# Delta pairs in slots: a pair's recurrence and the front of the next but one beside the inversion levels of the pair between

## The chip, the cores and the metric

The kernel runs on one core of a Trainium2 chip. The metric is the device time of one execution in microseconds (us). The engines are PE (TensorE; PEld is its weight load), DVE (VectorE), ACT (ScalarE), POOL (GpSimd) and SP (SyncE, which issues most of the DMAs). Each runs its own instructions strictly in the order of the program, and they meet only at semaphores.

## The reference, cut to what matters

One inference step of a two-layer decoder trunk runs over 1024 prompt tokens and eight sample tokens. The stage that the change is mainly about is the gated delta rule of the second layer: 8 heads, 64-token chunks, a 128x128 state per head. For each chunk it computes

```
m     = strict_lower(kb @ k^T * exp(gcum_i - gcum_j))
tinv  = inverse(eye + m);  u = tinv @ (v * beta);  w = tinv @ (kb * exp(gcum))
aqk   = lower(q @ k^T * exp(gcum_i - gcum_j))
v_new = u - w @ s
o     = (q * exp(gcum)) @ s + aqk @ v_new
s     = s * exp(g_last) + (k * exp(g_last - gcum))^T @ v_new
```

and then an rms norm of o times silu(z), and the output projection. Only s passes from chunk to chunk. The eight sample tokens make one step of the same rule on states of their own, which are read and written whole (4 MB). The first layer has an RWKV-7 recurrence of the same build (chunks of 64, an inversion, a state H), whose decay and gates are sigmoids.

## The kernel before

The kernel is a row of phases, one after the other: norm, projections, attention, `rwkv_phase`, an output projection (`residual_phase`), a convolutional feed-forward, norm, projections (`odd_phase`), `delta_phase`, `delta_samples_phase`, `residual_phase` again under the name `out1`, and a second feed-forward. The pages of the samples' attention are read and multiplied beside most of the first phases.

`delta_phase` takes the 16 chunks as 8 pairs; the two chunks of a pair lie in the partitions 0 to 63 and 64 to 127. Each engine has one loop over the pairs, and one body of the loop is one pair from start to end. A pair has three parts.

- The **front** loads q, k, v (`dn_x`), squares them (L2158), sums the squares with a matmul of ones (L2092), takes Ln and Exp for the norm (L2160, L2163), spreads the gates over partitions with a matmul (L2097), forms kb, kbe and qe on DVE (L2203 to L2206), transposes k and v (L2102), forms the decay differences (L2214 to L2220), `dn_bv` and `dn_ktm` (L2223, L2225), multiplies the three Gram blocks (L2112) and masks them (L2230 to L2240).
- The **levels** are the inversion: five times a group of 16 matmuls `y` (L1377), a copy on ACT (L1402), two such groups `z` and `zt` (L1388, L1394; the last level has only `zt`) and two subtractions on DVE (L1414, L1417). POOL multiplies the five masks (L2084) into a ring of five buffers.
- The **recurrence** goes twice, once for each chunk (`p`): kbe times state (L2129, semaphore `w_done`), state times qe (L2132), a subtraction on DVE (L2246, `r_ready`), the product with the inverse (L2137), a copy on ACT (L2179), the state's update (L2142 on PE, L2251 and L2254 on DVE), the output's part (L2145). Then the output is copied and squared (L2182, L2184), summed (L2150), normed (L2186, L2188, L2257) and multiplied with z into `T.h` (L2260).

`T.h` stays in SBUF until `out1` reads it. `delta_samples_phase` starts when `delta_phase` has ended: a load of the sample rows and the states, a turn through DRAM, two multiplications with a reduction each over 128 x 64 elements on DVE, another turn through DRAM, and a store of the states.

`rwkv_phase` is a loop over 8 pairs too, with the samples' pages as filling on DVE, ACT and PE. `prep_act` and `prep_dve` form the gates of a pair: Exp on ACT, then 1 + x and a reciprocal on DVE, for the pair `th`, `sg` (L1563 to L1566) and for the pair `rw`, `ra` (L1579 to L1582). The recurrence on PE has for each half 4 matmuls A times H (L1698) with 8 ak times v between them (L1701), 8 for the solution (L1707), 16 for the new state (L1714, L1716) and 20 for the output (L1720, L1724, L1726), and then a single `h_done`; DVE's update of H (L1855, L1862) waits for that.

The semaphore pattern that is spoken of below is this one in PE's program (L2148):

```
pe.wait_ge(S["o_sq"], i + 1)
for b in range(2):
    mm = pe.matmul(ps[:, b, :], ones, rs[:, 4 * b:4 * b + 4, :], start=True, stop=True)
mm.then_inc(S["o_sum"], 1)
```

## Time and profile before

| what | us |
|---|---|
| median of 3 runs | 5235.51 (5227.53 to 5235.9) |
| the profiled execution | 5225.01 |
| its span, first to last instruction | 5223.3 |
| `rwkv_phase` | 721 to 1988 |
| `delta_phase` | 3430.6 to 4166 |
| `delta_samples_phase` | 4166 to 4272 |
| `out1` | 4272 to 4379 |
| second feed-forward | 4379 to 5223 |

The phases don't overlap, so that the time is their sum. Over the whole span PE is busy 78%, DVE 51%, ACT 23% and POOL 5%, but those shares are means over phases with different limits.

### The profile page before, as it was taken

Reading aid. Unit: us, or ns where it says so; the run is one execution under the profiler, and the core shown is the slowest. Engines: PE = TensorE matmul, PEld = TensorE weight load, DVE = VectorE, ACT = ScalarE, POOL = GpSimd, SP = SyncE. Lnnn points to the kernel's source line nnn. Section 1 sums busy time; section 2 is a strip of 40 time slices with the busy share of each in tenths; the row PEclk is TensorE's granted clock in tenths of the full one; section 3 lists DMA queues with packets and bytes.
Section 4 is the critical chain, followed back from the end, with each engine's and each line's share of the span. In section 5 each row is a group of like instructions: output and inputs, shape, how many; then the busy total and the mean of one; then the engine's idle time right before and its main releaser. Section 6 shows DMA issues by size and latency. Waiting matters only on the chain. (4 is left out here: it accounts for less than half of the span.)

```text
span 5223.3 us, 83010 instructions
## 1 busy us (share of the span) xinstructions
PE 4090.6 (78%) x29517; PEld 3380.3 (65%) x29517; DVE 2662.9 (51%) x3402; ACT 1202.3 (23%) x1838; POOL 244.2 (5%) x302
## 2 busy tenths in 40 slices
PE   6787876776666777699999699966766626999998
PEld 6684333333333346699988688855656526999998
DVE  2157878888778823343434344444344362343433
ACT  3212541111111111222223222222121212222232
POOL 0000000000000000000000000001001000000000
PEclk8898987788867778899999899977777768999999
DMA  2252036777666632111134322211010113111154
GB/s 91 80 155 88 25 98 223 260 238 248 210 202 211 227 109 101 69 49 49 49 113 152 121 82 82 82 41 34 18 34 18 38 71 114 41 49 49 62 159 135
DMA packets 273719, 558.51 MB, mean 107 GB/s; under 512 B 35889, under 2 KB 93617, under 8 KB 266906
## 3 DMA queue, kind: packets, MB, share of 16 engines
q1 hardware_dynamic: 167434, 367.46, 22.0%
q10 hardware_dynamic: 90000, 141.65, 8.3%
q0 software_dynamic: 16032, 45.92, 2.2%
q8 instruction: 171, 2.80, 0.2%
q14 instruction: 82, 0.67, 0.0%
HBM read 500.74 MB, written 54.56 MB: 106 GB/s over the span
## 5 line engine op out<-in xcount | busy, mean ns | idle before, releaser
L260 PE MATMUL ps<-ffn_hh,up_wh 128*128 128x344 f32 x2112 | 678.0, 321 | 59.5 <-DVE up_wl L252 59.5
L262 PE MATMUL ps<-ffn_hl,up_wh 128*128 128x344 f32 x2112 | 676.3, 320 | 0.0
L261 PE MATMUL ps<-ffn_hh,up_wl 128*128 128x344 f32 x2112 | 675.6, 320 | 0.0
L1045 PE MATMUL ps<-pg_v,pg_w 128*8 128x512 f32 x1024 | 364.9, 724 | 133.7 <-DMA pg_v<-in_v_pages 106.0
L260 PEld LDWEIGHTS ps<-ffn_hh,up_wh 128*128 128x128 f32 x2112 | 398.2, 189 | 60.6 <-issue 60.6
L262 PEld LDWEIGHTS ps<-ffn_hl,up_wh 128*128 128x128 f32 x2112 | 398.2, 189 | 0.0
L261 PEld LDWEIGHTS ps<-ffn_hh,up_wl 128*128 128x128 f32 x2112 | 398.2, 189 | 0.0
L450 PE MATMUL ps<-down_ah,down_wh 128*128 128x344 f32 x1056 | 345.9, 328 | 52.1 <-DVE down_al L482 30.8
L1106 DVE TENSOR_TENSOR pg_prod<-pg_k,pg_q 128x1024 f32<-128x1024 f32 x256 | 316.0, 1235 | 47.9 <-DVE rw_mxt L1417 14.5
L451 PE MATMUL ps<-down_ah,down_wl 128*128 128x344 f32 x1056 | 339.1, 321 | 0.0
L452 PE MATMUL ps<-down_al,down_wh 128*128 128x344 f32 x1056 | 339.1, 321 | 0.0
L1110 DVE TENSOR_REDUCE pg_z<-pg_prod 128x16 f32<-128x1024 f32 (+1 forms) x256 | 312.7, 1221 | 11.4 <-DVE pg_prod L1106 0.2
L252 DVE TENSOR_TENSOR down_wl<-down_w,down_wh 128x1408 fp32r<-128x1408 f32 x96 | 155.9, 1624 | 312.5 <-ACT down_wh L247 312.5
L260 PE MATMUL ps<-hh,odd_wh 128*128 128x344 f32 x792 | 257.9, 326 | 65.0 <-DVE odd_wl L252 65.0
L1045 PEld LDWEIGHTS ps<-pg_v,pg_w 128*8 128x8 f32 x1024 | 42.3, 101 | 344.5 <-DMA pg_v<-in_v_pages 288.1
L261 PE MATMUL ps<-hh,odd_wl 128*128 128x344 f32 x792 | 254.3, 321 | 0.0
L262 PE MATMUL ps<-hl,odd_wh 128*128 128x344 f32 x792 | 254.3, 321 | 0.0
L450 PEld LDWEIGHTS ps<-down_ah,down_wh 128*128 128x128 f32 x1056 | 199.8, 189 | 66.5 <-issue 52.1
L247 ACT ACTIVATE down_wh<-down_w 128x1408 fp32r<-128x1408 f32 x96 | 132.4, 1379 | 368.5 <-PE ps L452 341.5
L451 PEld LDWEIGHTS ps<-down_ah,down_wl 128*128 128x128 f32 x1056 | 200.9, 190 | 0.0
L452 PEld LDWEIGHTS ps<-down_al,down_wh 128*128 128x128 f32 x1056 | 200.0, 189 | 0.0
L260 PEld LDWEIGHTS ps<-hh,odd_wh 128*128 128x128 f32 x792 | 149.9, 189 | 74.0 <-ACT odd_row L1954 43.9
(427 smaller groups left out, 7623.9 us busy)
## 6 DMA issues: line engine op xcount, KB each, us to landing
pg_k<-in_k_pages SPq DMA_DIRECT2D x512, 256.0 KB, 4.4
pg_v<-in_v_pages ACTq DMA_DIRECT2D x512, 256.0 KB, 4.7
down_w<-in_w_down SPq DMA_DIRECT2D x96, 704.0 KB, 4.1
up_w<-in_w_ff SPq DMA_DIRECT2D x44, 1034.0 KB, 4.8
odd_w<-in_w_odd SPq DMA_DIRECT2D x33, 526.0 KB, 4.0
scratch_odd_rows<-odd_cv POOLq DMA_DIRECT2D x32, 516.0 KB, 4.4
dn_x<-scratch_odd_rows SPq DMA_DIRECT2D x8, 1536.0 KB, 8.0
scratch_x<-out_x POOLq DMA_DIRECT2D x16, 516.0 KB, 2.9
```

The lines of the kernel that those rows point to most:

```text
L247: act.activation(hi, w, ACT.Copy).then_inc(rounded, 1)
L252: dve.tensor_tensor(lo, w, hi.bitcast(F32), ALU.subtract).then_inc(rest_ready, 1)
L260: pe.matmul(out, wh, xh, start=(k == 0), stop=False)
L261: pe.matmul(out, wl, xh, start=False, stop=False)
L262: mm = pe.matmul(out, wh, xl, start=False, stop=(k == n - 1))
L450: pe.matmul(ps[:, j, 0:GC], wh[:, v, wk], ah[:, kk, :], start=(kk == 0), stop=False)
L451: pe.matmul(ps[:, j, 0:GC], wl[:, v, wk], ah[:, kk, :], start=False, stop=False)
L452: mm = pe.matmul(ps[:, j, 0:GC], wh[:, v, wk], al[:, kk, :], start=False, stop=(kk == FT - 1))
L1045: pe.matmul(self.T.ps[c:c + H_A, 7, :], wts[:, :, g], self.vp[:, n, :], start=(g < 4), stop=(g >= NPG - 4), tile_position=(0, c), skip_gro ...
L1106: dve.tensor_tensor(self.prod[:, :, :], self.kp[:, n:n + 2, :], self.q[:, :].unsqueeze(1).to_broadcast([P, 2, D_A]), ALU.mult).then_inc(se ...
L1110: dve.tensor_reduce(z.rearrange("p h n -> p n h"), self.prod[:, :, :].rearrange("p n (h d) -> p n h d", h=H_A), AX.X, ALU.add).then_inc(se ...
```

## The change

The gates in `rwkv_phase` are formed by a minimum on DVE (`E_CAP` is 1e18), Ln with bias 1 on ACT and Exp of the negative on ACT; the fetch of sample pages in `prep_act` moves behind them:

```
+            act.wait_ge(S["gates_capped"], i + 1)
+            act.activation(th[0:64, 0:n], th[0:64, 0:n], ACT.Ln, bias=1.0)
+            act.activation(sg[:, 0:n], sg[:, 0:n], ACT.Ln, bias=1.0).then_inc(S["gates_log"], 1)
+            act.wait_ge(S["gates_log"], i + 1)
+            act.activation(th[0:64, 0:n], th[0:64, 0:n], ACT.Exp, scale=-1.0).then_inc(S["gates_rcp"], 1)
+            act.activation(sg[:, 0:n], sg[:, 0:n], ACT.Exp, scale=-1.0).then_inc(S["gate_in"], 1)
+            if sample is not None:
+                fetch(8)
...
+            act.wait_ge(S["capped"], i + 1)
+            act.activation(cut(t["rw"], n), cut(t["rw"], n), ACT.Ln, bias=1.0)
+            act.activation(cut(t["ra"], n), cut(t["ra"], n), ACT.Ln, bias=1.0).then_inc(S["w_log"], 1)
+            act.wait_ge(S["w_log"], 2 * i + 1)
+            act.activation(cut(t["rw"], n), cut(t["rw"], n), ACT.Exp, scale=-1.0)
+            act.activation(cut(t["ra"], n), cut(t["ra"], n), ACT.Exp, scale=-1.0).then_inc(S["w_log"], 1)
...
-            st.do(dve.tensor_scalar(th[0:64, 0:n], th[0:64, 0:n], 1.0, None, ALU.add))
-            st.link(dve.tensor_scalar(sg[:, 0:n], sg[:, 0:n], 1.0, None, ALU.add))
-            st.do(dve.reciprocal(th[0:64, 0:n], th[0:64, 0:n]))
-            dve.reciprocal(sg[:, 0:n], sg[:, 0:n]).then_inc(S["gate_in"], 1)
...
-            st.do(dve.tensor_scalar(cut(t["rw"], n), cut(t["rw"], n), 1.0, None, ALU.add))
-            st.link(dve.tensor_scalar(cut(t["ra"], n), cut(t["ra"], n), 1.0, None, ALU.add))
-            st.do(dve.reciprocal(cut(t["rw"], n), cut(t["rw"], n)))
-            st.link(dve.reciprocal(cut(t["ra"], n), cut(t["ra"], n)))
...
+            dve.tensor_scalar(th[0:64, 0:n], th[0:64, 0:n], E_CAP, None, ALU.min)
+            dve.tensor_scalar(sg[:, 0:n], sg[:, 0:n], E_CAP, None, ALU.min).then_inc(S["gates_capped"], 1)
...
+            dve.tensor_scalar(cut(t["rw"], n), cut(t["rw"], n), E_CAP, None, ALU.min)
+            dve.tensor_scalar(cut(t["ra"], n), cut(t["ra"], n), E_CAP, None, ALU.min).then_inc(S["capped"], 1)
...
+            dve.wait_ge(S["w_log"], 2 * i + 2)
```

The recurrence of `rwkv_phase` on PE is written in another order: the 16 ak times v ahead of the wait for `solved`, the output's own products behind `h_done`, with a new semaphore `mixed` that the copy of the output waits for:

```
+                for hd in range(8):
+                    for p in range(2):
+                        r = slice(64 * p, 64 * p + 64)
+                        pe.matmul(ps[r, 0, hc(hd)], ak[r, hc(hd)], vtm[r, hc(hd)], start=(hd == 0), stop=False,
+                                  skip_group_check=True)
+                pe.wait_ge(S["solved"], i + 1)
+                for p in range(2):
...
+                    for k in range(4):
+                        mm = pe.matmul(ps[r, 0, k * P:(k + 1) * P], t["A"][:, k, c], Hx[:, k, :, :], start=False, stop=True,
+                                       skip_group_check=True)
+                    mm.then_inc(S["w_done"], 1)
...
+                    alone(pe, S["pe_passed"])
+                    for hd in range(8):
+                        mm = pe.matmul(ps[q(hd), 2, hd // 2 * C:(hd // 2 + 1) * C], btm[r, hc(hd)], u[r, hc(hd)],
+                                       start=False, stop=True, skip_group_check=True)
+                    mm.then_inc(S["h_done"], 1)
+                    for hd in range(8):
+                        pe.matmul(ps[q(hd), 4, oc_(hd // 2)], vtm[r, hc(hd)], rk[r, hc(hd)], start=False, stop=False,
+                                  skip_group_check=True)
+                    for hd in range(8):
+                        mm = pe.matmul(ps[q(hd), 4, oc_(hd // 2)], u[r, hc(hd)], rb[r, hc(hd)], start=False, stop=True,
+                                       skip_group_check=True)
+                    mm.then_inc(S["mixed"], 1)
```

`delta_phase` and `delta_samples_phase` are replaced by two classes, `Delta` and `DeltaSamples`, whose methods are generators: a `yield` ends a slot. `abreast` runs the streams of an engine in turn, slot by slot, while the program is built, so that nothing is a loop on the chip any more. The outer stream holds fronts (4 slots) and recurrences (7 slots), the inner stream the levels (10 slots), the third stream the samples. In the steady state 11 slots hold the recurrence of pair k, then the front of pair k+2, and beside both the levels of pair k+1:

```
+    def outer(self, eng, head, front, recur):
...
+        yield from head(eng)
+        for n in range(2):
+            yield from front(eng, n)
+        for _ in range(self.B_SLOTS - self.A_SLOTS):
+            yield
+        for k in range(NPAIR):
+            yield from recur(eng, k)
+            if k + 2 < NPAIR:
+                yield from front(eng, k + 2)
+            elif k + 1 < NPAIR:
+                for _ in range(self.A_SLOTS):
+                    yield
...
+    def inner(self, eng, levels):
...
+        for _ in range(1 + self.A_SLOTS):
+            yield
+        for n in range(NPAIR):
+            yield from levels(eng, n)
+            for _ in range(self.R_SLOTS + self.A_SLOTS - self.B_SLOTS if n else 0):
+                yield
...
+def abreast(*streams):
...
+    live = list(streams)
+    while live:
+        live = [s for s in live if next(s, live) is not live]
...
+            abreast(D.outer(dve, D.head_dve, D.front_dve, D.recur_dve), D.inner(dve, D.levels_dve), N.dve(dve))
```

The methods hold the same operations as before, with these differences. `recur_pe` and `recur_dve` are the recurrence; the sums of squares and the square of the next front have slots of their own; the output goes to DRAM (`h_rows`), pair by pair, and z's buffer and the output's are single:

```
+    def pool(self, pool):
...
+        for n in range(NPAIR):
+            pool.wait_ge(S["blocks_copied"], n + 1)
+            for lv in range(1, 6):
+                k = 5 * n + lv - 1
+                if k >= 3:
+                    pool.wait_ge(S["y_done"], k - 2)
+                pool.tensor_tensor(self.h8(self.mtl[:, k % 3, :]), self.h8(self.mt[:, n % 2, :]), self.m8(f"lev{lv}T"), ALU.mult)\
+                    .then_inc(S["blocks_ready"], 1)
...
+    def front_pe(self, pe, n):
...
+        pe.wait_ge(S["keyed"], n + 1)
+        pe.wait_ge(S["tm_ready"], n + 1)
...
+    def recur_pe(self, pe, k):
...
+        pe.wait_ge(S["solved"], k + 1)
+        pe.wait_ge(S["blocks_copied"], min(k + 2, NPAIR))
+        if k:
...
+        for p in range(2):
...
+            pe.wait_ge(S["s_ready"], m + 1)
+            alone(pe, S["pe_passed"])
+            for hd in range(8):
+                mm = pe.matmul(ps[r, hd // 4, self.col(hd)], kbe[:, hd, c], st_[:, hd, :], start=True, stop=True)
+            mm.then_inc(S["w_done"], 1)
...
+        pe.wait_ge(S["o_sq"], k + 1)
+        pe.wait_ge(S["s_ready"], 2 * k + 3)
+        for i in range(2):
+            mm = pe.matmul(ps[:, i, :], T.const("ones"), self.rs[:, 4 * i:4 * i + 4, :], start=True, stop=True)
+        mm.then_inc(S["o_sum"], 1)
...
+        def store(n):
+            sp.wait_ge(S["out_ready"], n + 1)
+            sp.dma_start(T.h_rows[:, :, self.cols(n)].rearrange("t p n -> p t n"), self.o[:, :, :]).then_inc(S["out_stored"], 16)
+            if n + 1 < NPAIR:
+                sp.dma_start(self.Z[:, :, :], rows[:, 24:32, self.cols(n + 1)]).then_inc(S["z_in"], 16)
...
+        def load(n):
+            if n:
+                sp.wait_ge(S["gram"], 3 * n)
+            sp.dma_start(self.X[:, :, :], rows[:, 0:24, self.cols(n)]).then_inc(S["rows_in"], 16)
...
+    def recur_act(self, act, k):
...
+            act.wait_ge(S["mixed"], m + 1)
+            if k and not p:
+                act.wait_ge(S["out_stored"], 16 * k)
+            act.activation(o[:, :, c], ps[:, 2, :].rearrange("p (h i) -> p h i", h=8), ACT.Copy).then_inc(S["o_copied"], 1)
+            if p:
+                act.wait_ge(S["o_copied"], m + 1)
+                act.activation(rs[:, :, :], o[:, :, :], ACT.Square).then_inc(S["o_sq"], 1)
+                self.square_act(act, k + 2)
...
+    def out_dve(self, dve, k):
...
+        S, st, o = self.S, self.st, self.o
+        dve.wait_ge(S["rs"], k + 1)
...
+        dve.wait_ge(S["z_in"], 16 * k + 16)
+        st.link(dve.tensor_tensor(o[:, :, :], o[:, :, :], self.Z[:, :, :], ALU.mult))
+        dve.sem_inc(S["out_ready"], 1)
...
+    def front_dve(self, dve, n):
...
+        if n >= 2:
+            self.out_dve(dve, n - 2)
...
+        st.do(dve.tensor_tensor(h8(xt), h8(mt), m8("lev0T"), ALU.mult))
+        st.link(dve.tensor_tensor(h8(xm), h8(xm), m8("lev0"), ALU.mult))
+        st.do(dve.tensor_tensor(h8(xt), m8("eye64"), h8(xt), ALU.subtract))
+        st.do(dve.tensor_tensor(h8(xm), m8("eye64"), h8(xm), ALU.subtract))
+        st.link(dve.tensor_tensor(h8(at), h8(at), m8("inclT"), ALU.mult))
+        dve.sem_inc(S["x_begun"], 1)
...
+    def levels_dve(self, dve, n):
...
+            if lv < 5:
+                dve.wait_ge(S["z_done"], 4 * n + lv)
+                st.link(dve.tensor_tensor(xm, xm, ps[:, 5, :], ALU.subtract))
+                dve.sem_inc(S["xm_ready"], 1)
+            dve.wait_ge(S["zt_done"], 5 * n + lv)
+            st.link(dve.tensor_tensor(xt, xt, ps[:, 6, :], ALU.subtract))
+            dve.sem_inc(S["xt_ready"] if lv < 5 else S["solved"], 1)
+            yield
...
+    def recur_dve(self, dve, k):
...
+            dve.wait_ge(S["w_done"], m + 1)
+            st.link(dve.tensor_tensor(self.r0[r, :, :], self.bv[r, b, :, :],
+                                      ps[r, 0:2, :].rearrange("p b (h w) -> p (b h) w", h=4), ALU.subtract))
+            dve.sem_inc(S["r_ready"], 1)
```

The transposes of the gates' rows run once for all pairs (`head_pe`, `head_act`). `kbe`, `qe`, `ktm`, `bv`, `mt`, `xm`, `xt` and `at` have two buffers, the ring of masks three in place of five. In `DeltaSamples` the state is cut into 4 chunks of 16 columns, each in 6 slots of DVE's program:

```
+        for c in range(self.VC):
...
+            st.link(dve.tensor_tensor(t, s, k3, ALU.mult))
+            yield
+            st.link(dve.tensor_reduce(sa[:, :], over_k, AX.X, ALU.add))
...
+            yield
+            st.link(dve.tensor_tensor(t, k3, sa[:, :].unsqueeze(1).to_broadcast([P, P, 16]), ALU.mult))
+            yield
+            st.link(dve.scalar_tensor_tensor(out=s, in0=s, scalar=self.gr[:, 0:1], in1=t, op0=ALU.mult, op1=ALU.add))
+            yield
+            st.link(dve.tensor_tensor(t, s, q3, ALU.mult))
+            yield
+            st.link(dve.tensor_reduce(so[:, v], over_k, AX.X, ALU.add))
+            yield
```

`out1` reads its input back from DRAM, with 8 loads ahead of its first weights on SP's queue:

```
+            if src_in:
+                for k in range(KT):
+                    sp.dma_start(src[:, k, :], src_dram[k]).then_inc(src_in[k], 16)
...
+                if src_in:
+                    act.wait_ge(src_in[k], 16)
+                act.activation(sh[:, k, :], src[:, k, :], ACT.Copy).then_inc(src_rounded, 1)
```

How this moves instructions. First PE in the delta stage. Before, behind the last level of a pair came that pair's own recurrence, and nothing else:

```order
L1394 MATMUL ps<-dn_mxt,dn_my 64x64 x16
L2127 ISA
L2129 MATMUL ps<-dn_S,dn_kbe 64x128 x8
L2132 MATMUL ps<-dn_qe,dn_S 128x64 x8
L2137 MATMUL ps<-dn_r,dn_mxt 64x128 x8
L2142 MATMUL ps<-dn_vn,dn_ktm 128x128 x8
L2145 MATMUL ps<-dn_mat,dn_vn 128x64 x8
```

Now, on PE in the steady state, from the last Gram block of a front through the first chunk of a recurrence (L2282 to L2301) stand the next pair's levels (L2250 is y, L2260 and L2264 are z and zt):

```order
L2225 MATMUL ps<-dn_x 64x64 x16
L2282 MATMUL ps<-dn_state,dn_kbe 64x128 x8
L2287 MATMUL ps<-dn_qe,dn_state 128x64 x8
L2250 MATMUL ps<-dn_mxm,dn_mtl 64x64 x16
L2292 MATMUL ps<-dn_r,dn_mxt 64x128 x8
L2260 MATMUL ps<-dn_my,dn_mxt 64x64 x16
L2264 MATMUL ps<-dn_mxt,dn_my 64x64 x16
L2298 MATMUL ps<-dn_vn,dn_ktm 128x128 x8
L2301 MATMUL ps<-dn_mat,dn_vn 128x64 x8
```

Between the state's products and the product with the inverse there is now one group of a level, and behind that product there are two. Next, DVE in the same stage, over the last slot of a front and the first slots of the following recurrence, where the second row is one of the samples' (a reduction of a chunk):

```order
L2451 TENSOR_TENSOR dn_mat<-dn_mat,consts 128x512
L2651 TENSOR_REDUCE ds_so<-ds_t 128x16
L2475 TENSOR_TENSOR dn_r<-dn_bv,ps 64x1024
L2638 TENSOR_TENSOR ds_t<-ds_s,ds_kr 128x2048
L2479 TENSOR_TENSOR dn_tmp<-dn_state,dn_ee 128x1024
L2461 TENSOR_TENSOR dn_mxm<-dn_mxm,ps 128x512
L2464 TENSOR_TENSOR dn_mxt<-dn_mxt,ps 128x512
```

The subtraction that the recurrence starts with (L2475) now stands behind the masks of a front (L2447 to L2451) and, in the pairs that hold samples, behind a sample's operation. Last, PE in `rwkv_phase`. Before, from the end of A times H to the new state of a half:

```order
L1698 MATMUL ps<-rw_Hx,rw_A 64x128
L1701 MATMUL ps<-rw_mvtm,rw_mak 64x64 x2
L1707 MATMUL ps<-rw_mr,rw_mxt 64x64 x8
L1714 MATMUL ps<-rw_mvtm,rw_mktm 64x64
L1716 MATMUL ps<-rw_mu,rw_mbtm 64x64
```

Now, on PE, one whole half:

```order
L1723 MATMUL ps<-rw_Hx,rw_A 64x128 x4
L1727 MATMUL ps<-rw_R,rw_Hx 128x64 x4
L1732 MATMUL ps<-rw_mr,rw_mxt 64x64 x8
L1735 MATMUL ps<-rw_mvtm,rw_mktm 64x64 x8
L1740 MATMUL ps<-rw_mu,rw_mbtm 64x64 x8
L1744 MATMUL ps<-rw_mrk,rw_mvtm 64x64 x8
L1747 MATMUL ps<-rw_mrb,rw_mu 64x64 x8
```

The products that need no wait stand where the engine waits for a copy, and the output's last 16 stand behind those of the new state (L1740).

## Rows read from the trace of the kernel before

**Rows 1.** Windows: us, then busy (instructions) PE, PEld, DVE, ACT, POOL; clock; DMA share; GB/s

```profile
3430.00:4166.00 736.00, 501.55 (x6120) 427.33 (x6120) 296.56 (x312) 150.15 (x161) 64.42 (x41) 0.74 0.09 25
4166.00:4272.00 106.00, 7.36 (x37) 4.84 (x37) 64.05 (x13) 6.39 (x11) 0.00 (x0) 0.52 0.23 84
1231.00:1290.00 59.00, 48.89 (x527) 18.08 (x526) 50.00 (x46) 2.99 (x5) 0.00 (x0) 0.99 0.93 320
1290.00:1323.00 33.00, 29.62 (x243) 20.10 (x243) 24.85 (x26) 2.96 (x5) 0.00 (x0) 0.60 0.70 229
3750.00:3773.00 23.00, 17.84 (x397) 16.48 (x394) 6.56 (x9) 3.37 (x5) 0.00 (x0) 0.98 0.01 2
```

**Rows 2.** Timeline of SP: the stage's first load and the next stage's first

```profile
3430.64 0.40 SPq L2065 DMA_DIRECT2D dn_x<-scratch_odd_rows  x1
...
4272.35 0.37 SPq L297 DMA_DIRECT2D out_w<-in_w_out_odd  x1
```

**Rows 3.** Timeline of one pair's front (start, us, engine, operation, idle before it)

```profile
3710.55 1.89 ACT L2158 ACTIVATE dn_qk<-dn_x 128x2048 f32<-128x2048 f32 x1
...
3712.50 5.75 PE L2092 MATMUL ps<-dn_qk,ones_sb 128*128 128x512 f32 x8 [4.09 <-ACT dn_qk L2158]
...
3734.35 0.69 DVE L2230 TENSOR_TENSOR dn_mmt<-dn_mdt,ps 128x512 f32<-128x512 f32 x1 [0.31 <-DVE dn_ktm L2225]
...
3736.39 1.79 DVE L2234 TENSOR_TENSOR dn_mxt<-dn_mmt,consts 128x512 f32<-128x512 f32 x1 [0.15 <-DVE dn_mat L2232]
...
3743.38 1.97 PE L1377 MATMUL ps<-dn_mxm,dn_mtl 64*64 64x64 f32 x32 [11.05 <-DVEq L2238]
3743.43 1.42 DVE L2240 TENSOR_TENSOR dn_mat<-dn_mat,consts 128x512 f32<-128x512 f32 x1 [0.25 <-DVE dn_mxm L2237]
```

**Rows 4.** Timeline of the same pair's last levels and its recurrence

```profile
3762.11 1.15 PE L1377 MATMUL ps<-dn_mxm,dn_mtl 64*64 64x64 f32 x32
...
3766.21 1.96 PE L2129 MATMUL ps<-dn_S,dn_kbe 128*64 128x128 f32 x16 [1.03 <-DVEq L1418]
...
3770.03 1.96 PE L2137 MATMUL ps<-dn_r,dn_mxt 64*64 64x128 f32 x16
...
3773.18 2.38 PE L2142 MATMUL ps<-dn_vn,dn_ktm 64*128 64x128 f32 x16 [1.20 <-ACT dn_vn L2179]
...
3798.89 1.11 ACT L2186 ACTIVATE dn_rs<-ps,vecs_sb 128x1024 f32<-128x1024 f32 x1 [3.74 <-PE ps L2150]
...
3800.99 1.89 ACT L2158 ACTIVATE dn_qk<-dn_x 128x2048 f32<-128x2048 f32 x1
```

**Rows 5.** Groups of the delta stage: busy us, mean ns, idle before

```profile
L1377 PE MATMUL ps<-dn_mxm,dn_mtl 64*64 64x64 f32 x1280 | 57.8, 254 | 90.6 <-DVEq L2238 90.6
...
L1394 PE MATMUL ps<-dn_mxt,dn_my 64*64 64x64 f32 x1280 | 51.9, 237 | 6.2 <-ACT dn_my L1402 6.2
...
L1417 DVE TENSOR_TENSOR dn_mxt<-dn_mxt,ps 128x512 f32<-128x512 f32 x40 | 27.5, 687 | 33.1 <-PE ps L1394 33.1
...
L2112 PE MATMUL ps<-dn_kb,dn_qk 128*64 128x64 f32 x256 | 12.4, 270 | 0.7 <-DVEq L2207 0.6
```

**Rows 6.** Waits of DVE in the RWKV stage, then from 1860 to 1925 us

```profile
DVE rw_dh L1855 <- PE ps L1726: 77.5, 14, 16.2
...
DVE rw_dh L1855 <- PE ps L1726: 31.8, 2, 16.2
```

**Rows 7.** Groups of DVE in the RWKV stage

```profile
L1581 DVE RECIPROCAL rw_rw<-rw_rw 128x512 f32<-128x512 f32 (+1 forms) x9 | 27.2, 3020 | 0.3
```

**Rows 8.** DMA over two pairs: the queue that fetches instructions, and a load

```profile
q8 instruction: 17, 0.28, 0.6%
...
dn_x<-scratch_odd_rows SPq DMA_DIRECT2D x2, 1536.0 KB, 8.1
```

**Rows 9.** Eight loads in a row, of the norm after this stage

```profile
L199 SPq DMA_DIRECT2D normf_x<-scratch_x x8: 339/442/500, 4381.4 to 4384.7; - x8
...
DMA to landing us min/median/max: 3.6/6.5/9.2
```

More of the change, by code:

```diff
@@ L47 @@
 DECAY = float(np.exp(-0.5))
+E_CAP = 1e18
 EXP_LN_SET = "natural_log_exp_and_others"
@@ L282, in residual_phase @@
         sems(n) for n in ("product", "added", "stored", "x_free", "w_rounded", "w_split", "src_rounded", "src_split"))
+    src_in = [sems(f"src_in{k}") for k in range(KT)] if src_dram is not None else None
     with ExitStack() as ctx:
@@ L1708, in pair @@
                     mm.then_inc(S["u_done"], 1)
+                    for hd in range(8):
+                        pe.matmul(ps[q(hd), 2, hd // 2 * C:(hd // 2 + 1) * C], ktm[r, hc(hd)], vtm[r, hc(hd)],
+                                  start=(hd < 2), stop=False, skip_group_check=True)
                     pe.wait_ge(S["u_copied"], 2 * i + p + 1)
@@ L2062, in _ @@
+def abreast(*streams):
+    live = list(streams)
+    while live:
+        live = [s for s in live if next(s, live) is not live]
+def delta_phase(T, ba):
+    nc = T.nc
+    with ExitStack() as ctx:
+        state = ctx.enter_context(nc.sbuf_tensor("dn_state", [P, 8, P], F32))
+        D = Delta(T, ba, state, ctx)
+        N = DeltaSamples(T, ba, ctx)
+        block = ctx.enter_context(nc.Block())
         @block.sync
         def _(sp):
-            rows = T.odd_rows[0:32].rearrange("t p n -> p t n")
@@ L2072, in _ @@
-            sp.wait_ge(S["s_ready"], 2 * NPAIR + 1)
-            sp.dma_start(io["dn_prompt"], st_[:, :, :]).then_inc(S["state_out"], 16)
-            sp.wait_ge(S["state_out"], 16)
+            abreast(D.sp(sp), N.sp(sp))
         @block.gpsimd
         def _(pool):
-            pool.memset(st_[:, :, :], 0.0).then_inc(S["cleared"], 1)
-            pool.wait_ge(S["cleared"], 1)
-            pool.sem_inc(S["s_ready"], 1)
-            with pool.Fori(0, NPAIR) as i:
-                pool.wait_ge(S["blocks_copied"], i + 1)
-                for lv in range(1, 6):
-                    pool.tensor_tensor(h8(mtl[:, lv - 1, :]), h8(mt[:, :]), m8(f"lev{lv}T"), ALU.mult)\
-                        .then_inc(S["blocks_ready"], 1)
+            D.pool(pool)
@@ L2422, in trunk_program @@
                 odd_phase(T, ba)
-            with nc.sbuf_tensor("h1", [P, KT, TOK], F32) as T.h:
-                delta_phase(T, ba)
-                delta_samples_phase(T, ba)
-                residual_phase(T, "out1", io["w_out_odd"], T.h, x2, x3)
+            delta_phase(T, ba)
+        with nc.sbuf_tensor("h1", [P, KT, TOK], F32) as h:
+            residual_phase(T, "out1", io["w_out_odd"], h, x2, x3, T.h_rows)
         ffn(T, 1, x3, io["y"])
```

825 lines of the change are left out of this document (479 added, 346 removed).

## The prediction

> **What bounds the kernel now.** The phases follow each other, so each change is priced in its own phase and the differences are added. I read first the windows by stage, then the timeline of one delta pair, then the groups of that stage, then DVE's waits in the RWKV stage.
>
> The delta stage and the samples' stage together last from the first load to the first load of `out1`: 4272.35 - 3430.64 = 841.7 us [rows 2]. In the delta stage no engine is full: PE is busy 502 of 736 us, DVE 297, ACT 150 [rows 1]. What bounds it is that a pair is one chain. The reader is to see three lengths in the two timelines. The front lasts from the square at 3710.55 to the first level at 3743.38, 32.8 us [rows 3]. The levels last to 3766.21, 22.8 us, and the recurrence to the next pair's square at 3800.99, 34.8 us [rows 4]. Together 90.4 us a pair. The samples' stage has DVE at work in 64 of 106 us and PE in 7 [rows 1]: DVE's two passes over the states and DMA turns, with nothing beside them.
>
> In the RWKV stage DVE waits for the end of a recurrence half on PE: 77.5 us in 14 waits, of which 31.8 us are two waits in the last pair [rows 6]. The other twelve make 45.7 us. PE is 29.6 of 33 us busy in such a recurrence at a clock of 0.60, and the inversion beside it runs at 0.99 with the DMAs at 0.93 [rows 1].
>
> **The delta pairs in slots.** In the steady state a period holds a front and a recurrence in a row, and the 22.8 us of levels are spread beside them. The period is so the old front and the old recurrence, corrected for what is moved.
>
> Front: the square moves ahead, beside the last recurrence: its 1.95 us go (3710.55 to 3712.50 [rows 3]). The Gram products now wait for `dn_ktm`. Before, the masks started 0.31 us behind it [rows 3]; now three groups stand between, of which the first has 12.4 / 8 = 1.55 us [rows 5] and the others at most as much. I take 3.8 for the three, so +3.5. Two level subtractions of 0.69 [rows 5] stand ahead of kb on DVE, with a small copy: +1.6. Of the masks, four lay ahead of the first level, from 3736.39 to 3743.38, and the fifth (1.42) behind [rows 3]; now DVE's first subtraction of the recurrence stands behind all five. They are slow: 1.79 us for a 128x512 multiplication [rows 3], against 0.69 for one with a PSUM input [rows 5]; POOL multiplies its five masks just then. With the ring of three, POOL does three of them there and the other two later. I take 6.4 us in place of 6.9 (between 8.4, no relief, and 3.5, as quick as the 0.69 row): -0.5. Front: 32.8 - 1.95 + 3.5 + 1.6 - 0.5 = 35.5 us.
>
> Recurrence: from the state's first product to the product with the inverse it is 3770.03 - 3766.21 = 3.8 us [rows 4]. That product with the state now runs under the masks, and what is left is the subtraction behind them, about 1.3 (a 64x1024 operation, twice 0.69): -2.5. The end is where the first Ln of the output norm ends, 3800.00 [rows 4], since the ones-matmul of the next front needs only the bank: -1.0. On PE five pieces of levels come in (`y` 57.8 / 40 = 1.45, `z` and `zt` together 2.65 with 51.9 / 40 = 1.30 for one [rows 5]): behind each product with the inverse they take the place of a wait of 1.20 for ACT's copy [rows 4] (2.65 - 1.2 and 1.45 - 1.2), behind the first chunk's output and the second chunk's state products they come in whole (1.45 and 2.65), and at the end half a microsecond shows beside copy and square. Sum +6.3. Recurrence: 34.8 - 2.5 - 1.0 + 6.3 = 37.6 us. **Period 73 us** against 90.4.
>
> The whole stage: load 8.1 [rows 8], first front with its square 37.5, second front with two levels beside it 38, three levels alone at 22.8 / 5 = 4.6 each, 14: 97 us. Then six periods, 438. Then the recurrence of the seventh pair beside the last levels, 38, the last recurrence with its two multiplications, 37.5, and two half-megabyte transfers, 8.5 by the quick end of such loads (3.6, [rows 9], plus the issues): 84.
>
> Samples: DVE's 64 us [rows 1] lie in 24 slots of its program. In ten of those DVE is on the chain (a front's four slots and the one behind it): 64 x 10 / 24 = 27. Some 4 us of a period there DVE waits for ACT or PE anyway, twice: 19 us remain. Bounds 0 and 64. The turns through DRAM lie beside five or more slots.
>
> Sum 97 + 438 + 19 + 84 = 638 us, against 841.7: **-204**.
>
> Costed at nothing: a pair's load of q, k, v, issued when the Gram products are done. It lands 8.1 us later [rows 8] and is squared six slots later, more than 30 us; if SP came to it late (the store of the output and z's load stand ahead in its queue, and wait for DVE's last multiplication), each microsecond beyond the 20 or so to spare would be one on the period. POOL's masks make 64.4 / 8 = 8 us a period [rows 1], needed over nine slots. The new wait of ACT for the output's store comes in the third slot of the next recurrence, four slots behind the store; behind it stand only the copies of that chunk.
>
> A rule against this. DVE's rescaling of the state, with two SBUF inputs, now can meet POOL's last two masks. The Trainium skill, "SBUF — State Buffer", section "SBUF: two separate sides", says that DVE and GpSimd share a port pair as an exclusive lock, and that a DVE operation with two SBUF inputs waits whole for a GpSimd operation that reads SBUF. The trace agrees in kind with 1.79 against 0.69 [rows 3, 5]. By the rule 16 rescalings could each be late by a POOL mask of 1.6 us (a fifth of those 8), 26 us; by the rows each by 1.1, 18 us. I take none, as the rescaling stands where DVE waits for PE; the range covers either.
>
> **out1** reads its input back. Eight loads take 3.3 us to issue and the last lands 4384.7 + 9.2 - 4381.4 = 12.5 us after the first was issued [rows 9]; the weights come behind. Before, the input was in SBUF and only the weights were waited for, about 3.6 us for such a load [rows 9], and ACT and PE start with the first piece. **+11** (8 to 16).
>
> **RWKV.** On the chain of a half, 4 products of R and H, 16 output products, 8 of ak and v and 8 of the new state move off to places where PE waits or to behind `h_done`. By the nearest rows (1.3 to 1.45 us for 16 small ones [rows 5], more at the clock of 0.60) that is 4.2 to 6 us a half, more than the mean wait of 45.7 / 12 = 3.8: those go. In the last pair, with nothing beside it, 2 x 5.3 go. The output's copy comes later by 16 products, which is covered in part: +6 over the stage. The gates: two reciprocals of 3.0 us a pair [rows 7] leave DVE, and ACT gets four operations of some 0.6 (half of 1.11 for twice the columns [rows 4]) in the chain; with the other DVE work behind, I take -1.3 a pair (0 to -3.3), -10. Sum -45.7 - 10.6 + 6 - 10 = **-60** (-25 to -85: should the pages' DMAs at 0.93 set the pace, DVE's waits only move).
>
> **Sum.** -204 + 11 - 60 = -253. The durations are of the profiled execution of 5225 us; this gives 4972, predicted as **4970 us**. The median of before is 10 us above that execution, 0.2%, which is also about what a measurement of this kernel can tell from no change.
>
> **The rivals.** *TensorE at its lower level.* Of the 73 us some 42 are PE: the 37.6 less the subtraction (1.3), copy and square (2 x 1.1 [rows 4]) and Ln (1.1), plus 5.75 for the sums of squares [rows 3] and the 3.8 of the Gram groups. Its groups show both levels: 1.97 us for a `y` at 3743.38, right after 11 us of idleness [rows 3], and 1.15 at 3762.11 [rows 4], with the mean at 1.45 [rows 5]. All at the slower: 42 x (1.97 / 1.45 - 1) = +15, a period of 88, so nearly nothing from the overlap. Over eight periods' worth of work that is +120: 5090. For it: 0.60 in the busy RWKV recurrence; against it: 0.98 in levels and recurrence of this stage [rows 1]. *The upper level, and all waits gone.* 42 x (1 - 1.15 / 1.45) = 9 off, a period of 64, -72, and up to 22 more in the RWKV stage: 4875 to 4900. For it: PE's idle stretches, after which it is slow, get shorter. *Slower than before: instruction fetch.* Nothing is a loop any more. Two pairs before fetched 17 blocks [rows 8], 8.5 a pair: 0.6% of 16 engines over the 182 us of that view is 17 us, so about one for a block. All 253 us would be eaten from 32 us a pair on, some 3.7 us of bare stall a block. Against it: the loops' bodies are fetched anew in every pair already. The Trainium skill, "Runtime: NRT & Kernel Launch", section "Instruction fetch mechanics", says that the sequencer streams 16 KiB blocks ahead and that a taken branch breaks this; by that rule the straight code gains. *No change:* only if the slots don't overlap, each stream waiting for the other in turn; the orders of PE and DVE speak against it.
>
> **How the numbers follow.** Forecast 0.68 (4920 to 5020 as its own range), lower level 0.14, upper level 0.14, slower 0.03, no change 0.01. The range 4880 to 5080 leaves out half of the first rival, a third of the second and the last two, under 0.2. Faster by over 0.2%: 0.96; within: 0.01; slower: 0.03.
>
> **What would show it.** The delta stage from its first load to `out1` near 640 us, with a square every 73 us; POOL's masks split three and two; DVE's idle time before the update of H near zero except in the last pair; the first matmul of `out1` some 11 us later behind its loads. Wrong would be: a period near 64 or 88 with the clock to match, DVE busy without a gap in the pairs with samples (then the 19 is too small), or fetches ahead of idle PE.

## The result

The changed kernel takes 4941.9 us in the median of four runs (4933.8 to 4945.3), the kernel before 5231.6: a ratio of 0.944, 95% interval 0.943 to 0.946. The forecast was 4970 us: the gain is 290 us, where the sum had 253 and this median less the forecast gives 262. By stages, from the two profiled executions, which lie 283 us apart (each stage from its first load to the next one's):

| stage | before | after | difference | forecast |
|---|---|---|---|---|
| RWKV | 1269.2 | 1195.8 | -73.4 | -60 |
| delta and samples | 841.7 | 624.4 | -217.3 | -204 |
| `out1` | 109.0 | 119.0 | +10.0 | +11 |
| all the rest | 3003.3 | 3001.3 | -2.0 | 0 |

A second profile of the changed kernel, from a later set of runs, has 1201.0, 608.3 and 118.9 us in the first three rows: the stages of one profile are good to some 5 us for RWKV and 16 us for the delta stage, while the medians of the two sets lie within 3 us of each other.

The windows of the RWKV stage, of the delta stage and of one period of it, in the changed kernel (columns as in rows 1):

```profile
716.00:1912.00 1196.00, 799.90 (x7548) 396.54 (x7548) 872.52 (x954) 219.54 (x423) 66.68 (x44) 0.81 0.68 222
3354.00:3978.00 624.00, 489.32 (x6157) 433.65 (x6156) 347.98 (x352) 154.22 (x177) 58.73 (x41) 0.77 0.18 50
3663.00:3736.00 73.00, 60.74 (x832) 55.00 (x831) 41.67 (x47) 22.14 (x24) 7.60 (x5) 0.85 0.20 52
```

Beside rows 1: the delta stage holds the same PE work, but in 624 us at a mean clock of 0.77 in place of 736 at 0.74 plus 106 of samples, and in a stretch of 73 us without samples the clock is 0.85 and PE busy 61. SP's timeline shows the periods, since a pair's load is issued when the Gram products of the pair before it are done:

```profile
3353.72 0.40 SPq L2134 DMA_DIRECT2D dn_x<-scratch_odd_rows  x1
...
3527.25 0.37 SPq L2134 DMA_DIRECT2D dn_x<-scratch_odd_rows  x1
...
3612.28 0.37 SPq L2134 DMA_DIRECT2D dn_x<-scratch_odd_rows  x1
...
3681.88 0.37 SPq L2134 DMA_DIRECT2D dn_x<-scratch_odd_rows  x1
...
3746.59 0.37 SPq L2134 DMA_DIRECT2D dn_x<-scratch_odd_rows  x1
...
3814.73 0.37 SPq L2134 DMA_DIRECT2D dn_x<-scratch_odd_rows  x1
...
3978.12 3.90 SPq L297 DMA_DIRECT2D h<-scratch_h_rows  x8
```

Between the loads lie 85.0, 69.6, 64.7 and 68.1 us; the first of those holds the most sample work. `out1` starts at 3978.12 with its eight loads. One period without samples, on PE and DVE:

```profile
3683.93 1.80 DVE L2447 TENSOR_TENSOR dn_mxt<-dn_mmt,consts 128x512 f32<-128x512 f32 x1 [0.15 <-DVE dn_mat L2445]
3683.93 1.93 PE L2282 MATMUL ps<-dn_state,dn_kbe 128*64 128x128 f32 x16 [2.08 <-issue]
...
3689.59 0.68 DVE L2451 TENSOR_TENSOR dn_mat<-dn_mat,consts 128x512 f32<-128x512 f32 x1
...
3690.43 1.22 DVE L2475 TENSOR_TENSOR dn_r<-dn_bv,ps 64x1024 f32<-64x1024 f32 x1 [0.15 <-DVE dn_mat L2451]
...
3692.07 3.40 PE L2292 MATMUL ps<-dn_r,dn_mxt 64*64 64x128 f32 x15
...
3700.24 1.89 PE L2301 MATMUL ps<-dn_mat,dn_vn 64*128 64x64 f32 x16
...
3703.14 1.96 PE L2282 MATMUL ps<-dn_state,dn_kbe 128*64 128x128 f32 x16
...
3717.68 1.98 PE L2307 MATMUL ps<-dn_rs,ones_sb 128*128 128x512 f32 x4
...
3721.08 3.67 PE L2195 MATMUL ps<-dn_g,ones_sb 128*128 128x512 f32 x8 [0.33 <-ACT dn_rs L2376]
```

The order is the one forecast: the product with the state (L2282) runs under DVE's masks, the recurrence's subtraction (L2475) stands behind the five of them, and levels lie between its steps. The masks last from 3683.93 to 3690.3, 6.4 us, as forecast. What differs from the forecast is PE: the output's products (L2301) take 1.89 us in each chunk, the output's sums (L2307) 1.98 and the second chunk's product with the state (L2282, the one at 3703.14) 1.96. The same three in the pair of rows 4, before the change, are slower:

```profile
3775.36 3.51 PE L2145 MATMUL ps<-dn_mat,dn_vn 64*128 64x64 f32 x16
...
3778.80 3.26 PE L2129 MATMUL ps<-dn_S,dn_kbe 128*64 128x128 f32 x16
...
3795.20 3.65 PE L2150 MATMUL ps<-dn_rs,ones_sb 128*128 128x512 f32 x4 [2.20 <-ACT dn_rs L2184]
```

The granted clock in three stretches of the changed kernel says why (columns as in rows 1): the product with the inverse behind the wait for the masks, which takes 3.6 us (L2292: the row has 15 of its 16; 1.96 in rows 4); the last levels and the output's sums of this period; and the same groups one period later.

```profile
3692.10:3695.00 2.90, 2.90 (x19) 2.90 (x16) 0.92 (x1) 0.60 (x1) 1.72 (x1) 0.50 0.03 6
3715.60:3719.60 4.00, 4.00 (x71) 2.63 (x70) 1.37 (x2) 3.45 (x3) 0.00 (x0) 1.00 0.02 4
3781.20:3787.00 5.80, 5.80 (x69) 4.52 (x68) 1.38 (x2) 3.45 (x3) 0.00 (x0) 0.57 0.01 3
```

The first stands at the lower of the two levels (0.50 is 1.2 GHz), the second at the upper, the third near the lower again, and that period is 3.4 us longer (68.1 against 64.7).

Where samples lie beside it (a period of 85 us), the same step looks like this on DVE and PE:

```profile
3535.86 3.58 DVE L2651 TENSOR_REDUCE ds_so<-ds_t 128x16 f32<-128x2048 f32 x1 [0.15 <-DVE dn_mat L2451]
...
3548.59 3.62 DVE L2640 TENSOR_REDUCE ds_sa<-ds_t 128x16 f32<-128x2048 f32 x1 [0.15 <-DVE dn_mxt L2464]
...
3555.33 3.65 PE L2282 MATMUL ps<-dn_state,dn_kbe 128*64 128x128 f32 x16 [2.84 <-DVEq L2484]
```

A sample's reduction of 3.6 us (L2651) stands between the masks and the subtraction, and another (L2640) between the state's product and the state's sum. PE waits for both, 3.0 us for the first and 2.84 for the second, and the product behind the second wait takes 3.65 us where it took 1.96 above. Over that period the granted clock is 0.68, against 0.87 in the one without samples.

DVE's waits in the RWKV stage, beside rows 6:

```profile
DVE rw_yw L1592 <- PE ps L1512: 41.3, 9, 4.6
...
DVE rw_A L1577 <- ACTq L1568: 21.6, 8, 2.8
...
DVE rw_L L1602 <- ACT rw_ra L1552: 19.2, 8, 2.5
...
DVE rw_dh L1876 <- PE ps L1740: 14.3, 2, 9.5
```

The wait for the recurrence's half fell from 77.5 us to 14.3, all of it in the last pair. In its place DVE waits longer for the gates (41 us where it was 30), 19 us for ACT's Ln and Exp ahead of the scan, and 22 us for the decays that ACT forms behind the scan (L1568). Before the change DVE was idle for 0.3 us at each of the last two places.

### The profile page after: what moved, and what is told of

Same layout as the page of the kernel before. It is cut to its first block and busy times, and to the rows that moved or that the text cites. A ratio compares the mean times of both kernels' runs of the same rounds, so it can differ in the third digit from the quotient of the medians.

```text
span 4940.5 us, 82596 instructions
## 1 busy us (share of the span) xinstructions
PE 4001.3 (81%) x29517; PEld 3331.4 (67%) x29517; DVE 2583.9 (52%) x3393; ACT 1226.2 (25%) x1915; POOL 238.8 (5%) x302
## 5 line engine op out<-in xcount | busy, mean ns | idle before, releaser
L1052 PE MATMUL ps<-pg_v,pg_w 128*8 128x512 f32 x1024 | 382.8, 721 | 155.6 <-DMA pg_v<-in_v_pages 104.0
```

The source lines that it names most:

```text
L1052: pe.matmul(self.T.ps[c:c + H_A, 7, :], wts[:, :, g], self.vp[:, n, :], start=(g < 4), stop=(g >= NPG - 4), tile_position=(0, c), skip_gro ...
```

## The experiments

Each ratio is to the kernel before on the same chip.

**The RWKV order alone** (the kernel before with the hunks of the diff on PE's recurrence and the semaphore `mixed`).

> The kernel before with the new order of PE in the RWKV recurrence alone (new semaphore mixed, ak times v ahead of solved); gates and delta stage as before. Theory: most of the 73 us that left the RWKV stage are DVE's waits for the end of a recurrence half, 77.5 us before and 14.3 after; alone this gives -45 to -60 us, 5172 to 5187 against 5232, and the two updates of H in a pair stand 12 us apart in place of 17.3. Rival: the gates' reciprocals were the larger part; then this alone gives less than -30 (above 5200).

Measured: 5166.5 us, ratio 0.9867 (0.985 to 0.9883), -69 us. DVE's waits:

```profile
DVE rw_yw L1574 <- PE ps L1505: 30.3, 9, 4.3
...
DVE rw_dh L1859 <- PE ps L1723: 13.3, 2, 8.6
```

The half's wait is down to 13.3 us, and the wait for the gates stays at the 30 us of before. The stage itself is 1205.0 us, 64 less than before, so the order is nearly all of the stage's gain, and it is more than the 45 to 60 expected here: the two updates of a pair stand 12.1 us apart in place of 17.3, and a pair lasts 146 in place of 153 us.

**The gates alone** (the hunks with `E_CAP`, Ln and Exp).

> The kernel before with the gates formed by Ln and Exp on ACT alone; recurrence and delta stage as before. Theory: -10 to -28 us (5204 to 5222), since the reciprocals (6 us a pair on DVE) give way to a chain of four ACT operations. Rival: more than -40 (below 5190), if the reciprocals were the larger part of the 73 us, or no change, if DVE's gain is eaten by its new waits for ACT (19 us for the scan in the changed kernel).

Measured: 5228.3 us, ratio 0.9989 (0.9977 to 1.0001): -6 us, which can't be told from nothing. The reciprocals of the stage, 69 us of DVE's work before, left DVE, but its waits for the gates, the decays and ACT's Ln and Exp are as long as those above, 59 us more than before (7 of them for the first gate's Exp).

**The delta stage alone** (all hunks but those two).

> The delta stage with samples in slots and the reload of the input in out1, without either edit of the RWKV stage. Theory: the parts add up, -217 + 10 = -207 us, 5020 to 5030 against 5232. Rival: the parts share something (the clock or the transfers of the sample pages), then it is off by more than 15 us from that.

Measured: 5016.0 us, ratio 0.9581 (0.9564 to 0.9597), -220 us. That is 13 us more than the -207 expected, and the stage is 612 us in this profile; the two profiles of the changed kernel have 624 and 608. The three parts sum to -69 - 6 - 220 = -295 us, and together they gave 290: they add up.

**The streams of a pair in a row.**

```
-        for n in range(2):
-            yield from front(eng, n)
...
+        for n in range(NPAIR):
+            yield from front(eng, n)
+            for _ in range(self.B_SLOTS):
+                yield
+            yield from recur(eng, n)
```

(the waits and loads that follow from it are moved along).

> The changed kernel with the streams of a pair in a row: front, levels and recurrence of pair n, then those of pair n+1, straight code, same buffers and engines' operations, samples still in slots beside them. Theory: the gain is the overlap of levels with recurrence and front; then a pair costs 88 to 95 us again and the stage 760 to 820 us in place of 624, 5080 to 5140 in all. Rival: the gain is that the code is straight, the output leaves by DRAM and the samples lie beside the pairs; then at most 60 us of it are lost (below 5005).

Measured: 5129.0 us, ratio 0.9788 (0.9771 to 0.9804), the stage 803 us. A pair without samples costs 90 to 97 us. So straight code, the way over DRAM and the samples beside the pairs together give 38 us of the stage's 217, and the overlap of the streams 179. Groups of PE in this kernel (busy us, mean ns of one):

```profile
L2290 PE MATMUL ps<-dn_mat,dn_vn 64*128 64x64 f32 x256 | 53.6, 396 | 0.0
...
L2296 PE MATMUL ps<-dn_rs,ones_sb 128*128 128x512 f32 x32 | 30.3, 1101 | 14.2 <-ACT dn_rs L2359 14.2
```

and the same lines in the changed kernel, with the product with the inverse:

```profile
L2292 PE MATMUL ps<-dn_r,dn_mxt 64*64 64x128 f32 x256 | 41.8, 330 | 5.1 <-DVEq L2477 5.1
...
L2301 PE MATMUL ps<-dn_mat,dn_vn 64*128 64x64 f32 x256 | 35.5, 297 | 0.0
...
L2307 PE MATMUL ps<-dn_rs,ones_sb 128*128 128x512 f32 x32 | 19.1, 727 | 1.8 <-ACT dn_rs L2372 1.8
```

The same instructions take 396 and 1101 ns with the streams in a row, and 297 (L2301) and 727 ns (L2307) with other work packed around them; over the stage the granted clock is 0.70 there and 0.77 in the changed kernel. The rival, straight code as the cause, is out.

**The samples behind the pairs.**

```
-            abreast(D.outer(dve, D.head_dve, D.front_dve, D.recur_dve), D.inner(dve, D.levels_dve), N.dve(dve))
+            abreast(D.outer(dve, D.head_dve, D.front_dve, D.recur_dve), D.inner(dve, D.levels_dve))
+            abreast(N.dve(dve))
```

and so on each engine.

> The changed kernel with the samples' stream behind the pairs' streams, as a stage of its own again (state still in 4 chunks). Theory: in the slots the samples cost about 22 us, the three periods that hold them taking 69, 85 and 69.5 us against 67 without; behind the pairs they cost their old 106 us, so +80 to +95 us, 5022 to 5037, and all six periods last 65 to 69 us. Rival: the long period of 85 us and the slow start have another cause (the clock, which is 0.71 there); then a period near 85 stays and the loss is 105 us or more.

Measured: 5026.6 us, ratio 0.9601 (0.9585 to 0.9617), +85 us. The loads of the pairs now:

```profile
3518.82 0.37 SPq L2134 DMA_DIRECT2D dn_x<-scratch_odd_rows  x1
...
3586.68 0.37 SPq L2134 DMA_DIRECT2D dn_x<-scratch_odd_rows  x1
...
3654.68 0.37 SPq L2134 DMA_DIRECT2D dn_x<-scratch_odd_rows  x1
...
3721.60 0.37 SPq L2134 DMA_DIRECT2D dn_x<-scratch_odd_rows  x1
...
3786.24 0.37 SPq L2134 DMA_DIRECT2D dn_x<-scratch_odd_rows  x1
```

Periods of 67.9, 68.0, 66.9 and 64.6 us: the long period of 85 us was the samples'. From the first recurrence to the seventh it takes 391.8 us here and 424.4 in the changed kernel (418.7 in its second profile), and to the first recurrence 99.3 against 106.7 (103.6): in the slots the samples cost 31 to 40 us, by the one profile or the other, not the 19 of the forecast and not the 22 expected here.

**The samples only in slots 1 to 6** (five more empty slots behind each chunk, seven ahead of the first, and the later steps moved back by 27).

> The changed kernel with the samples' six operations of a chunk only in the slots 1 to 6 of four recurrences, none in a front's slots or the one behind. Theory (the price comes from the ten slots in which DVE is on the chain): 10 to 20 us less, 4922 to 4932. Rival: DVE's in-order operations of 2.2 to 3.6 us delay the state's update and the subtractions just as much there; then no gain or a loss, 4937 to 4960.

Measured: 4933.4 us, ratio 0.9428 (0.9411 to 0.9445), 9 us less, within the noise and short of the 10 to 20 expected. The periods that hold samples last 64.7 to 66.9 us, so there the price is gone (387 us for the six, against 392 with no samples beside them), but the end behind them is 112 us in place of 93: PE waits there 12.7 us for the samples, as the run of the two edits below shows.

**POOL's masks later.**

```
-            pool.wait_ge(S["blocks_copied"], n + 1)
+            pool.wait_ge(S["x_begun"], n + 1)
```

> The changed kernel with POOL waiting for x_begun in place of blocks_copied, so that its five masks begin when DVE's five have ended. Theory (the two engines hold each other up over the same operands): the three slow masks of DVE fall from 1.6 to 1.8 us to 0.68, x_begun and the recurrence's first subtraction come 3 us earlier in each of 8 fronts, and the first group y only 1.6 us later relative to it, beside that subtraction: 10 to 25 us less, 4917 to 4932. Rival: the masks are slow for their own operands (two in SBUF, one broadcast), or the first group of the next levels, later by POOL's first mask, sets the pace: 4940 or more.

Measured: 4918.9 us, ratio 0.9393 (0.9377 to 0.9408), -23 us, the stage 586 us (624 and 608 in the profiles of the changed kernel). POOL's masks, DVE's first mask and the rescaling of the state, first in the changed kernel:

```profile
L2171 POOL TENSOR_TENSOR dn_mtl<-dn_mmt,consts 128x512 f32<-128x512 f32 x40 | 58.1, 1465 | 489.9 <-DVEq L2446 339.0 <-PE ps L2250 150.9
...
L2479 DVE TENSOR_TENSOR dn_tmp<-dn_state,dn_ee 128x1024 f32<-128x1024 f32 x16 | 20.6, 1291 | 1.9 <-DVE dn_r L2475 0.3
...
L2447 DVE TENSOR_TENSOR dn_mxt<-dn_mmt,consts 128x512 f32<-128x512 f32 x8 | 13.3, 1656 | 1.2 <-DVE dn_mat L2445 1.2
```

and with the masks later:

```profile
L2171 POOL TENSOR_TENSOR dn_mtl<-dn_mmt,consts 128x512 f32<-128x512 f32 x40 | 55.8, 1413 | 459.9 <-DVEq L2452 349.5 <-PE ps L2250 110.4
...
L2479 DVE TENSOR_TENSOR dn_tmp<-dn_state,dn_ee 128x1024 f32<-128x1024 f32 x16 | 23.2, 1452 | 1.9 <-DVE dn_r L2475 0.3
...
L2447 DVE TENSOR_TENSOR dn_mxt<-dn_mmt,consts 128x512 f32<-128x512 f32 x8 | 5.5, 693 | 1.2 <-DVE dn_mat L2445 1.2
```

DVE's mask falls from 1656 to 693 ns with the same operands, only because POOL no longer works beside it; the rescaling rises from 1291 to 1452, since POOL's masks now meet that. The rival, slow operands, is out. The Trainium skill, "SBUF — State Buffer", section "SBUF: two separate sides", has a DVE operation with two SBUF inputs wait for a GpSimd operation that reads SBUF. The trace agrees in kind; in size each of the three slow masks was 0.8 to 1.0 us late, less than one POOL mask (1.27 us in the median). The price was on the masks, not on the rescalings, for which the prediction had weighed it: those took 1291 ns in the changed kernel and 1225 before, 1 us over all 16.

**The reload from ACT's queue.**

```
-                    sp.dma_start(src[:, k, :], src_dram[k]).then_inc(src_in[k], 16)
+                    act.dma_start(src[:, k, :], src_dram[k]).then_inc(src_in[k], 16)
```

> The changed kernel with the eight loads of the reload in out1 issued from ACT's queue, so that the first weights on SP's queue no longer stand behind them. Theory: the +10 us of out1 is the order of the queue; the weights land about 4 to 6 us after issue and the first pieces with them: 5 to 9 us less, 4933 to 4937. Rival: the eight loads of half a megabyte fill the DMA engines, and the last of them, 12 us on, still sets the first product's end: no change within 2 us.

Measured: 4943.9 us, ratio 0.9438 (0.9421 to 0.9456): no change. `out1` is 115.7 us in place of 119.0. ACT's timeline there:

```profile
3991.78 4.45 ACTq L313 DMA_DIRECT2D h<-scratch_h_rows  x8
3996.90 1.06 ACT L248 ACTIVATE out_wh<-out_w 128x1024 fp32r<-128x1024 f32 x1 [15.49 <-DMA out_w<-in_w_out_odd]
...
4001.72 1.06 ACT L318 ACTIVATE out_sh<-h 128x1032 fp32r<-128x1032 f32 x1 [1.50 <-DMA h<-scratch_h_rows]
```

In the changed kernel ACT had waited for the weights, which stood behind the eight loads, until 14 us after the first issue, and then took all pieces without a wait:

```profile
3992.08 1.06 ACT L248 ACTIVATE out_wh<-out_w 128x1024 fp32r<-128x1024 f32 x1 [24.32 <-DMA out_w<-in_w_out_odd]
```

So there the order of the queue made the first matmul late: it comes 17.6 us into the stage, against 7.3 before the change and 8.7 in this run. But with the weights there after 5 us the pieces come one by one, with up to 1.5 us of waiting ahead of each, and the stage gets back only 3.3 of its 10 us: the rest is that waiting, 5.5 us in all, and the 1.4 us by which the first matmul is later than before the change.

**Work for PE ahead of the inverse.**

```
+            if not p:
+                for _ in range(4):
+                    pe.matmul(ps[:, 3, :], T.const("ones"), T.const("sel")[:, 0:512], start=True, stop=True)
```

> The changed kernel with four 128x512 matmuls of constants into an unused bank, in every recurrence behind the first chunk's products of the state, where PE waits some 2.7 us for DVE's masks. They add work whose result nothing reads. Theory (the periods came out at 65 to 68 us and not at 73 because PE's groups ran nearer the upper clock, and what is slow yet is slow behind a wait): the group behind (3.6 us for the product with the inverse, against 1.9 where PE was busy before) falls to about 2, and the period by 1 to 3 us: 4920 to 4937 against 4942 on the chip of the first runs. Rival: the group is slow for its operands, or the four matmuls push it back: no gain, 4940 to 4965.

Measured: 4935.9 us, ratio 0.9434 (0.9418 to 0.945), against 0.9442 for the changed kernel on that chip: no gain that can be told. Groups of PE:

```profile
L2295 PE MATMUL ps<-dn_r,dn_mxt 64*64 64x128 f32 x256 | 30.7, 270 | 3.3 <-DVEq L2480 3.3
```

The product with the inverse falls from 330 to 270 ns in the mean; each of its 16 groups now takes 1.9 us, where six took 3.6, and the clock in the one at 3690 us is 1.00:

```profile
3690.00:3691.90 1.90, 1.90 (x29) 1.90 (x27) 0.00 (x0) 0.60 (x1) 1.26 (x1) 1.00 0.00 0
```

That part of the theory holds. The time doesn't follow; the periods without samples last 64.7 to 66.6 us. PE's timeline in the one that begins with DVE's mask at 3680.10 shows why:

```profile
3685.42 3.65 PE L2290 MATMUL ps<-consts,ones_sb 128*128 128x512 f32 x8
...
3689.98 1.80 PE L2295 MATMUL ps<-dn_r,dn_mxt 64*64 64x128 f32 x15
```

The masks end at 3686.5, but the added matmuls hold PE until 3689.0. The product with the inverse starts 9.9 us after the first mask, where it started 8.1 us after it in the changed kernel, and ends 11.8 us after it in both. The next period is alike; in the one behind it 1.4 us are gained. So in two of these three the second half of the rival holds: the four matmuls push the group back by about as much as it gets faster.

**Two edits, three edits, and the changed kernel again.**

> The changed kernel with POOL's masks behind x_begun and the samples' operations in the slots 1 to 6. Theory (the masks' price and the samples' price lie on different slots and add up): 24 + 18 us less in the delta stage, near 582 us for it, and 4895 to 4910 in all. Rival: with the masks moved into the recurrence, POOL and the samples' operations of two SBUF inputs meet there and hold each other up; then less than 30 us of the 42 come.

> The same with the reload of out1 issued from ACT's queue too. Theory: out1 is 116 us in place of 119 and the whole 3 us less than with the two edits, if that can be seen at all. Rival: no difference, or slower by the 4.5 us that ACT needs to issue them.

> The changed kernel itself, unaltered, to have it on the same chip as the three above. Both theories: 4935 to 4955 us and a ratio of 0.943 to 0.946 to the kernel before, the delta stage at 624 us.

Measured: 4921.9 us, 0.941 (0.9394 to 0.9425), for the masks and the samples' slots together; 4921.7 us, 0.9415 (0.9389 to 0.9441), with the reload too; 4939.6 us, 0.9442 (0.9427 to 0.9458), for the changed kernel. So the two give 18 us, not 42, and no more than the masks alone: the stage is 585 us in this profile and 586 there. The six periods take 374 us, against 398 with the masks alone and 387 with the slots alone, so the two edits do add up there; the loss is at the end, 107 us against 87 with the masks alone. PE's timeline in the last pair's recurrence:

```profile
3904.92 1.02 PE L2573 MATMUL ps<-consts,ds_orow 8*128 8x8 f32 x8 [14.26 <-DMA ds_orow<-scratch_dn_o]
```

PE waits 14.3 us for the samples' last turn through DRAM, which I had moved back with the rest into the last recurrence; that pair's product with the inverse stands behind it on PE, and takes 3.67 us there and 1.93 with the masks alone. An earlier place for that step, with room behind the stores, wasn't tried. The three versions with the masks later (4919, 4922 and 4922 us) can't be told apart; all are some 20 us below the changed kernel.

## Why the prediction was right, point by point

*The chain of a pair.* Right: front and recurrence in a row, levels between. Without the overlap the stage loses 179 of its 217 us.

*The period, 73 us.* Mis-sized: 65.3 in the mean of the six in the run with the samples behind the pairs. The term that was too large is PE's share, taken at the durations that PE had in that pair of the kernel before. In the period shown above the two output products are 2 x 1.62 us shorter than in the pair of before, the output's sums 1.7, the sums of squares 2.1 (3.67, against 5.75 in rows 3) and the second chunk's product with the state 1.3, while the first chunk's product with the inverse is 1.7 longer: 6.6 of the 7.7 us. The second rival, the upper level, gave a period of 64 and was nearer than the forecast's 73, though pieces behind a wait stay slow. So the period itself was forecast wrongly, and the total is right partly because other errors go the other way.

*The samples, 19 us.* Mis-sized the other way: 31 to 40. I had counted only the ten slots of the fronts. In the recurrence's slots, too, a reduction of 3.6 us delays the state's sum; in the slots 1 to 6 alone this costs next to nothing, so most of it is in the slots of the front and the one behind it, the ten that the forecast had priced at 27 before it took 8 off. The lower clock in those periods (0.68 in the longest) is part of the price; how much of it wasn't separated.

*Start and end, 97 and 84 us.* They took 107 and 93 in the profiled run (104 and 86 in the second). Without samples the start is 99.3. The end differs between the two profiles by the clock of the last recurrence, 0.56 and 0.69.

In the profiled run the errors are -46 for the six periods, +14 for the samples in them (32.6 against 19), +10 at the start and +9 at the end: -13 in all, and the stage came out at 624 where 638 was forecast. Part of that closeness is luck: they cancel.

*The masks and the shared operands.* The 6.4 us of the five masks are as forecast; that they could fall to 3.5 stood there as a bound, and the run with the masks later reaches it (3744.46 to 3747.7, 3.2 us).

*`out1`, +11 us.* Right in size (+10.0), and the first matmul comes 10.3 us later into the stage, behind the loads, as forecast. The rows named for it give only 12.5 - 3.6 = 8.9, so the 11 was partly a guess. With the loads on the other queue the first matmul is early, and most of the price stays.

*RWKV, -60 us.* Right in mechanism, short in size: the order alone -69 where -45.7 - 10.6 + 6 = -50 was forecast. A half got 5.2 us shorter, within the 4.2 to 6 of the forecast. That the +6 for the output's copy didn't come, and that the first halves begin earlier, can each be a part of the 19 us more; no run separates them. The gates, -10, gave -6, which is not clear of nothing: the chain of four ACT operations was in the forecast, the wait for the decays behind it was not.

*Instruction fetch.* The straight code of the kernel with streams in a row costs no more than some 5 us a pair over the loop (95 against 90.4, and a part of that is the Gram products behind `dn_ktm`); the break-even of 32 us is far off. In the delta and samples' stages together 70 blocks of instructions were fetched before and 49 in the changed kernel.

## What to carry to other kernels

When a serial chain is broken into streams, price the new period with the durations that PE has between other work, not with those of a trace full of waits: here that was most of 8 in 73 us. Work that is put beside a chain on an in-order engine costs only where the engine is on the chain, so place it there by slot, and place its later waits too: a DRAM turn that landed in the wrong slot made PE wait 14 us, most of what the better places had won. Where two engines read SBUF at once, look at which of them is on the chain and let the other one go later; the name of one semaphore was worth 23 us here.

## What the runs showed of the hardware that was not expected

The clock fell where PE had no wait at all. In the period of 68.1 us the granted clock is 0.57 in the stretch from 3781.2 to 3787.0, with PE busy all of it and in the groups ahead, and 1.00 in the same groups one period earlier; from the output's products to its sums that is 8.9 us in place of 5.8, 3.1 of the 3.4 us that the period is longer. The second profile of the changed kernel has the same 68.1 us there, while the run of the delta stage alone, with the same code in that stage, has 64.8; what decides it stays open. The 16 us between the two profiles of the changed kernel lie elsewhere: 3 in the start, 5 in the first period (clock 0.80 and 0.87) and 7 in the last recurrence (0.56 and 0.69).

The price of DVE and POOL at work on SBUF side by side fell on DVE: three of its masks took 1.5 to 1.7 us each beside POOL and 0.69 without it. POOL's masks fell only from 1465 to 1413 ns in the mean when they were moved, though they then meet DVE's rescaling.
